# Zero products in TensorE's waits, halves side by side in the feed-forward, and the order of sums and norm steps

## What is computed

```python
# first block, per layer l (x: sequence, y: context)
hx = _rmsnorm(x, norm_g[l]) * (1.0 + scale) + shift      # scale, shift, gate: silu(c) @ w_mod[l] + b_mod[l]
f_in, f_gate, g_u, g_v, g_gate, c_q, c_kv, k_rope, a_gate = _split_in(h @ w_in)
f_out = (_fourier(f_in) @ w_fmix) * silu(f_gate)
g_out = _spatial_gate(g_u, g_v, g_ln_g, g_ws, g_bs) * silu(g_gate)
q  = _rmsnorm(c_q, q_a_g) @ w_uq                          # latents: their sums of squares
kv = _rmsnorm(c_kv, kv_a_g) @ w_ukv
x  = x + gate * (concat([fx, gx, attention * silu(ax)]) @ w_out[l])

# second block
u = a * sigmoid(b)                                        # a, b from x @ w_in
u = depthwise_conv(u, conv_w) + conv_b                    # 31 taps
y_conv = silu(layer_norm(u, conv_ln_g, conv_ln_b)) @ w_conv_out
merged = g_attn * y_attn + g_conv * y_conv                # y_attn: dilated window attention, three groups
x = layer_norm(alpha * x + merged @ w_o, ln1_g, ln1_b)
x = layer_norm(alpha * x + (silu(x @ w_gate) * (x @ w_up)) @ w_down, ln2_g, ln2_b)
```

## Time and profile before

| what | value |
|---|---|
| median of 3 runs | 924.92 us |
| the profiled execution | 929.94 us |
| its span, first to last instruction | 928.1 us |
| mean granted clock of TensorE | 0.983 |
| TensorE busy | 879.0 us, 95% |
| TensorE weight loads | 724.3 us, 78% |
| VectorE busy | 612.8 us, 66% |
| ScalarE busy | 427.1 us, 46% |
| DMA, mean over the span | 147 GB/s |

### The profile page before, as it was taken

One profiled execution on the slowest core, in us unless ns is written; L12 is line 12 of the kernel. 1 busy time (PEld: TensorE's weight loads), 2 busy tenths in 40 slices (PEclk: granted clock), 3 DMA queues, 4 the chain that ended last, 5 costly groups with the idle time before them and its releaser, 6 DMA issues.

```text
span 928.1 us, 13761 instructions
## 1 busy us (share of the span) xinstructions
PE 879.0 (95%) x5592; PEld 724.3 (78%) x5592; DVE 612.8 (66%) x1200; ACT 427.1 (46%) x711; POOL 21.2 (2%) x16
## 2 busy tenths in 40 slices
PE   4899999999999999999999999988999799999996
PEld 1468477767687767877998888887999699999995
DVE  3442666575845759865699999967586845544555
ACT  3342515544633355554544444556453744444441
POOL 0000000000000000000003113000000000000000
PEclk9999999999999999999999999989999899999999
DMA  9666352100263033203555665522366255455541
GB/s 349 261 226 245 143 215 84 46 23 1 91 249 120 12 125 137 83 21 136 162 190 177 200 192 173 158 81 69 101 199 218 73 195 188 172 186 204 178 163 46
DMA packets 39999, 136.71 MB, mean 147 GB/s; under 512 B 4352, under 2 KB 4480, under 8 KB 39680
## 3 DMA queue, kind: packets, MB, share of 16 engines
q1 hardware_dynamic: 38928, 130.48, 41.1%
q10 hardware_dynamic: 1008, 5.36, 1.5%
HBM read 134.77 MB, written 1.05 MB: 146 GB/s over the span
## 4 chain that ended last, share of the span: by engine, by line
PE 79%; DVE 15%; ACT 3%; issue 1%; DMA 1%; DVEq 0%; SPq 0%; ACTq 0%
PE ps L349 9%; PE ps L350 9%; PE ps L354 8%; PE ps L903 6%; PE ps L419 4%; PE ps L421 4%; PE ps L420 4%; PE ps L447 3%; PE ps L679 3%; DVE wlo L1391 2%; PE ps L377 2%; PE ps L702 2%; PE ps L379 2%; PE ps L378 2%; PE ps L366 2%; PE ps L368 1%
## 5 line engine op out<-in xcount | busy, mean ns | idle before, releaser
L1391 DVE TENSOR_TENSOR wlo<-raw,whi 128x1024 fp32r<-128x1024 f32 (+2 forms) x204 | 233.8, 1159 | 38.4 <-ACT whi L941 38.3
L941 ACT ACTIVATE whi<-raw 128x1024 fp32r<-128x1024 f32 (+2 forms) x204 | 204.4, 1005 | 104.0 <-DMA raw<-wpack 46.9
L349 PE MATMUL ps<-hh,whi 128*128 128x256 f32 (+1 forms) x736 | 217.3, 295 | 3.0 <-ACT AF L1264 2.5
L350 PE MATMUL ps<-hl,whi 128*128 128x256 f32 (+1 forms) x736 | 213.4, 290 | 0.0
L354 PE MATMUL ps<-hh,wlo 128*128 128x256 f32 (+1 forms) x640 | 185.7, 290 | 0.0
L349 PEld LDWEIGHTS ps<-hh,whi 128*128 128x128 f32 x736 | 141.9, 193 | 8.3 <-issue 4.8
L350 PEld LDWEIGHTS ps<-hl,whi 128*128 128x128 f32 x736 | 142.0, 193 | 3.0 <-issue 0.7
L354 PEld LDWEIGHTS ps<-hh,wlo 128*128 128x128 f32 x640 | 123.4, 193 | 1.4
L419 PE MATMUL ps<-whi,hh 128*128 128x512 f32 (+1 forms) x192 | 70.8, 369 | 0.2 <-ACT acc L1007 0.2
L420 PE MATMUL ps<-wlo,hh 128*128 128x512 f32 (+1 forms) x192 | 70.2, 366 | 0.0
L421 PE MATMUL ps<-whi,hl 128*128 128x512 f32 (+1 forms) x192 | 70.2, 366 | 0.0
(11 more groups left out here) (267 smaller groups left out, 1554.5 us busy)
## 6 DMA issues: line engine op xcount, KB each, us to landing
raw<-wpack SPq DMA_DIRECT2D x178, 512.0 KB, 4.1
AF<-wmod SPq DMA_DIRECT2D x48, 512.0 KB, 6.1
raw<-wpack SPq DMA_DIRECT2D x24, 256.0 KB, 2.7
XT<-xin SPq DMA_DIRECT2D x4, 512.0 KB, 6.1
raw<-wpack SPq DMA_DIRECT2D x4, 432.0 KB, 5.1
uq<-wuq ACTq DMA_DIRECT2D x2, 768.0 KB, 5.7
cst<-cpack ACTq DMA_DIRECT2D x1, 1093.0 KB, 8.0
AF<-wukv ACTq DMA_DIRECT2D x2, 512.0 KB, 7.0
```

The source lines that it names most:

```text
L349: e.matmul(o, wh[:, b], xh(k), start=j == 0, stop=False, skip_group_check=True)
L350: e.matmul(o, wh[:, b], xl(k), start=False, stop=False, skip_group_check=True)
L941: e.activation(W.hi(i), W.raw(i), ACT.Copy).then_inc(*HI.up(j))
L1391: e.tensor_tensor(W.lo(i), W.raw(i), W.hi(i), ALU.subtract).then_inc(*LO.up(j))
```

## The change

It has five parts.

1. `keep(n)` issues n products of a zeroed 128 x 256 tensor `K.zero` into a PSUM bank that nobody reads: 15 before the first product, 5 behind `mod_t(0, 0)`, 11 behind the first layer norm's sums. VectorE zeroes the tensor first of all.
2. The latents' sums are issued from within `lin_tm`, behind its second weight group of three.
3. `hh` and `hl` become two halves of one tensor `hx`. In chunks 1 to 21 of the feed-forward `lin_wide` takes both as one moving operand of 2 x 256 columns, so the high-by-high and high-by-low parts land in two halves of a bank. ScalarE copies the second half out, and VectorE adds the first half to it, for the gate and for the up projection.
4. Steps of the convolution's norm go to later items: sums 3 to 4, mean 3 to 4, centring 4 to 5, squares (ScalarE) 4 to 6, sum of squares 4 to 7, token sums 5 to 8, roots 5 to 8, spread 6 to 9, and `conv_act` is cut into steps of two channel groups each: scale in 10 and 11, tanh in 11 and 12, product in 12 and 13, high part in 13 and 14, low part in 14 and 15. The squares get four buffers in place of two.
5. In layer 0, VectorE's `bias(0, 5)` is done ahead of `kv_take(0, 0)`.

```diff
+    def lin_wide(key, wname, cols, xw):
+
+        free = ps.take(key)
+        c, wh, wl = weights(key, (wname, 0, tuple(range(KD)), cols), KD * P)
+        pe.wait_ge(*free)
+        for k in range(KD):
+            b = slice(k * P, (k + 1) * P)
+            pe.wait_ge(xw(k))
+            e.matmul(ps.ap(key, 512).rearrange("p (s n) -> p s n", s=2), wh[:, b], K.hx[:, :, k, 0:256], start=k == 0, stop=False, skip_group_check=True)
+            i = e.matmul(ps.ap(key, 256), wl[:, b], hh[:, k, 0:256], start=False, stop=k == KD - 1, skip_group_check=True)
+        i.then_inc(*M.up(key))
+        W.given[c] = M.now()
...
-    def lin_tm(key, wname, l, cols, n, xh, xl, tiles, per, xw, side=None):
+    def lin_tm(key, wname, l, cols, n, xh, xl, tiles, per, xw, side=None, mid=None):
...
+            if mid and g == per:
+                mid()
...
+    def keep(n):
+
+        pe.wait_ge(V["zero"], *ps.take("keep"))
+        for _ in range(n):
+            e.matmul(ps.ap("keep", 256), K.zero[:, 0:P], K.zero[:, :], start=True, stop=True, skip_group_check=True)
+
+
+    keep(15)
     pe.wait_ge(K.c0["cst"])
     mod_g(0, 2, 0)
...
     mod_t(0, 0)
+    keep(5)
...
+        lin_tm((l, "gvkr"), "w_in", l, (("gvkr",), 288), 288, XH, XL, tiles, 3, ht, side=(l, "kf") if l else None, mid=latent_sums)
...
-        if i == 3:
+        if i == 4:
             conv_sums()
-        if i == 5:
+        if i == 8:
             token_sums(("cn2",), 2)
-        if i == 6:
+        if i == 9:
             spread(("cn2",), 256)
...
     ln_sums("ln1")
+    keep(11)
...
-            lin(("fg", f), "w_ffn_gate_2", 0, cc, range(KD), x2h, x2l, 256, xt3)
-            lin(("up", f), "w_ffn_up_2", 0, cc, range(KD), x2h, x2l, 256, xt3)
+            lin_wide(("fg", f), "w_ffn_gate_2", cc, xt3)
+            lin_wide(("up", f), "w_ffn_up_2", cc, xt3)
...
+            e.activation(side[:, 0:256], ps.ap(("fg", m), 256, 256), ACT.Copy).then_inc(*A.up(("fgs", m)))
+            ac.wait_ge(V["fga", m])
+            e.activation(K.AF[:, z:z + 256], side[:, 0:256], ACT.Silu).then_inc(*A.up(("fg", m)))
         highs(("up", m))
+        if m:
+            ac.wait_ge(M["up", m])
+            e.activation(side[:, 256:512], ps.ap(("up", m), 256, 256), ACT.Copy).then_inc(*A.up(("ups", m)))
...
+            dv.wait_ge(A["fgs", m])
+            e.tensor_tensor(side[:, 0:256], side[:, 0:256], ps.ap(("fg", m), 256), ALU.add).then_inc(*V.up(("fga", m)))
+            ps.give(("fg", m), V.now())
+            dv.wait_ge(A["ups", m])
+            e.tensor_tensor(side[:, 256:512], side[:, 256:512], ps.ap(("up", m), 256), ALU.add).then_inc(*V.up(("upa", m)))
+            ps.give(("up", m), V.now())
+            dv.wait_ge(V.now(), A["fg", m], V["f", m - 2] if m >= 2 else None)
+            e.tensor_tensor(h, K.AF[:, z:z + 256], side[:, 256:512], ALU.mult).then_inc(*V.up(("fu", m)))
...
+        for m in range(4):
+            if i == 10 + m // 2:
+                conv_scale(m)
+            if i == 12 + m // 2:
+                conv_silu(m)
+            if i == 14 + m // 2:
+                conv_low(m)
```

More of the change, by code:

```diff
@@ L552, in layer, with latent_sums @@
             pe.wait_ge(*ps.take((l, "kf")))
[L553 to L563, removed]
+        def latent_sums():
+            pe.wait_ge(*free_st, A[l, "cqsq", 1])
+            for t in tiles:
+                for m in range(2):
+                    j = (t - tiles[0]) * P
+                    i = e.matmul(ps.ap(st, 1, t), K.sq[:, m * 512 + j:m * 512 + j + P], C("ones", 0, 1), start=m == 0, stop=m == 1, skip_group_check=True)
+            i.then_inc(*M.up((l, "cqsum")))
+            pe.wait_ge(A[l, "ckvsq"])
+            for t in range(4):
+                i = e.matmul(ps.ap(st, 1, 4 + t), K.acc[:, t * P:(t + 1) * P], C("ones", 0, 1), start=True, stop=True, skip_group_check=True)
+            i.then_inc(*M.up(st))
+        lin_tm((l, "gvkr"), "w_in", l, (("gvkr",), 288), 288, XH, XL, tiles, 3, ht, side=(l, "kf") if l else None, mid=latent_sums)
         ps.drop(st)
@@ L1359, in scalar_program @@
         highs(("fg", m))
+        side = K.AF[:, 8192 + 2 * z:8704 + 2 * z]
         ac.wait_ge(M["fg", m], V["fu", m - 2] if m >= 2 else None)
-        e.activation(K.AF[:, z:z + 256], ps.ap(("fg", m), 256), ACT.Silu).then_inc(*A.up(("fg", m)))
-        ps.give(("fg", m), A.now())
+        if m == 0:
+            e.activation(K.AF[:, z:z + 256], ps.ap(("fg", m), 256), ACT.Silu).then_inc(*A.up(("fg", m)))
+            ps.give(("fg", m), A.now())
+        else:
+            e.activation(side[:, 0:256], ps.ap(("fg", m), 256, 256), ACT.Copy).then_inc(*A.up(("fgs", m)))
+            ac.wait_ge(V["fga", m])
+            e.activation(K.AF[:, z:z + 256], side[:, 0:256], ACT.Silu).then_inc(*A.up(("fg", m)))
         highs(("up", m))
+        if m:
+            ac.wait_ge(M["up", m])
+            e.activation(side[:, 256:512], ps.ap(("up", m), 256, 256), ACT.Copy).then_inc(*A.up(("ups", m)))
         ac.wait_ge(V["fu", m], M["fd", m - 8, 1] if m >= 8 else None)
@@ L1461, in make_h @@
         h_low(l, ks[-1])
+    e.memset(K.zero, 0.0).then_inc(*V.up("zero"))
     e.memset(K.c32[:, :], 0.0).then_inc(*V.up("c32z"))
@@ L1658, in heads_T @@
             ps.give(key, V.now())
+        if l == 0:
+            bias(0, 5)
         kv_take(0, 0)
         if l == 0:
-            bias(0, 5)
             hsum("k", 0, 0, 0, 0)
@@ L1948, in vector_program @@
                 add_up(g.CV[:, k, :], k == 0, ("cn", "acc"), M["h", 1, "s"])
-        if i == 4:
+        if i == 5:
             conv_centre()
-        if i == 5:
+        if i == 7:
+            conv_squares()
+        if i == 8:
             rstd(("cn2",), 2, 512, LN_EPS)
-        if i in (7, 8, 9, 10):
-            conv_act(i - 7)
+        for m in range(4):
+            if i == 10 + m // 2:
[4 more added lines that the diff above has]
+                conv_low(m)
         if i == 12:
@@ L2019, in vector_program @@
         h = K.AF[:, 512 + z:768 + z]
[L2020 to L2022 removed]
+        side = K.AF[:, 8192 + 2 * z:8704 + 2 * z]
+        if m == 0:
+            dv.wait_ge(M["up", m], A["fg", m])
+            e.tensor_tensor(h, K.AF[:, z:z + 256], ps.ap(("up", m), 256), ALU.mult).then_inc(*V.up(("fu", m)))
+            ps.give(("up", m), V.now())
+        else:
+            dv.wait_ge(A["fgs", m])
[3 more added lines that the diff above has]
+            e.tensor_tensor(side[:, 256:512], side[:, 256:512], ps.ap(("up", m), 256), ALU.add).then_inc(*V.up(("upa", m)))
+            ps.give(("up", m), V.now())
+            dv.wait_ge(V.now(), A["fg", m], V["f", m - 2] if m >= 2 else None)
+            e.tensor_tensor(h, K.AF[:, z:z + 256], side[:, 256:512], ALU.mult).then_inc(*V.up(("fu", m)))
         dv.wait_ge(A["f", m])
```

37 lines of the change are left out of this document (21 added, 16 removed).

## The result

The changed kernel takes 913.63 us (median of 4 runs, 909.82 to 914.79) against 925.03 (4 runs, 924.67 to 926.61), 11.4 us less by the medians. The ratio of the means is 0.9866, 95% interval 0.9835 to 0.9898, or 12.4 us less (9.4 to 15.3). The forecast was 904.0, its range 898 to 911: the sign is right, and the time lies 9.6 us above the forecast. The profiled execution took 914.21. The mean granted clock of the four runs was 0.991, 0.992, 0.991 and, in the run of 909.82, 0.995: one of the four had clearly less low clock than the profiled one.

What follows compares the result with a forecast made beforehand. TensorE, busy nearly all the span, was taken as the bound, losing time to half rate and waits; -5.2 - 0.5 - 1.7 - 1.7 - 8.2 - 3.6 = -20.9 took 929.94 to 909.0, the median 924.92 to 904.0, range 898 to 911.

Steps and rivals of the forecast that it cites:

- The norm: Convolution's norm, items 3 to 11: later steps remove waits and low clock, -8.2, between -4 and -9.2.
- rival (b): Convolution's norm: VectorE bounds items 5 to 13, price 4.2, giving 908; chance 0.16.
- (c): Opening and gap before the feed-forward: the zeros don't lift the clock, giving 914; chance 0.09.
- the opening's term: Kernel start: 15 zero products bring what follows to full rate, 5.7 saved, 0.5 given back, -5.2.
- (d): Feed-forward: ScalarE and VectorE handovers never overlap, 9.9 an item against 8.5, slower at 937; chance 0.03.
- The halves: Feed-forward, 21 items: three 256-column products become one of 512 and one of 256, 10.5 ns a step, -3.6.
- keep(11): Gap behind the first layer norm's sums: 11 zero products speed the products behind, 0.4 to 0.7, taken as -0.5.
- the bound of -8: Feed-forward halves: the gain if the whole 13 ns of a second start went too.
- my plain row: Feed-forward halves: the plain 512-column product, 0.229 each, taken as the two-range product's cost, giving -3.6.
- the bound from L629: Feed-forward halves: two-range products at 0.891 against 0.86 cost 8 ns more, which leaves -0.8.
- nothing, if the clock falls elsewhere: Latents' sums, layers 0 and 1: the no-gain case against the forecast -1.7 and -1.7.
- Rival (a): Latent sums and convolution's norm: low clock comes back elsewhere, up to 6.7, giving 910.7; chance 0.20.

Runs made afterwards that it cites:

- the earlier trace: The kernel before, unchanged: the profiled execution that the forecast was built on, 929.94 us.
- the repeat: The kernel before, unchanged, profiled once more: 925.16 us, one execution.

## Why the prediction was right or wrong

**Right.** *The norm.* -8.2 forecast, -8.0 measured alone (-6.4 to -9.4); 41 us forecast for items 3 to 11, 39.9 found. The waits of 2.4 and 2.5 are gone, and the new one at the values is 0.7 where I put 1.0. That the two totals agree so closely is partly luck: the profile saves 9.4 in the items and loses 1.0 behind them. *VectorE* has 31.27 of 39.9 busy and TensorE all of it, so rival (b) did not happen. *Zeros lift the clock*: fifteen take 8.24, where at half rate they would take about 12.9 and at full rate about 6.4, so (c) falls. The 5.7 of the opening's term supposed that everything behind the zeros would run at full rate. No row of before showed that; the changed kernel does, with 1.90 for the second two modulation groups (3.62 in the earlier trace rows) and 1.12 for the spread (2.08). How many of the fifteen would go at half rate was an estimate of mine that no row of before shows; 8.24 fits some four of them (8.24 less 15 x 0.43 is 1.8, four times 0.43), with an end at 9.4. *The feed-forward's copies and sums*: VectorE 91.84 and ScalarE 82.80 in 18 items are 5.1 and 4.6 an item (forecast 5.2 and 4.7), and TensorE never waits, so (d) falls. *Layer 1's sums*: -1.7 forecast, -1.6 in the table, and none of the six profiles with the sums in the groups has the fall, against six of the eight with the sums behind them.

Whether zeros would lift the clock at all was open when the prediction was made. The runs answer it: fifteen products took 8.24 to 9.49 with zeros and 8.84 with ones, each far below the 12.9 of half rate.

**Mis-sized.** *The halves*: a step was to fall from 0.359 to 0.349 and measured (8.387 - 2.74) / 16 = 0.353, 6 ns of the 10.5. By the earlier trace rows one start is 10 ns (twice 5.75 / 48 less 2.75 / 12) where I had about 13, and the bound of -8, which uses the 13, would be -7. The direct term, -2.5 over 21 items, lies between my plain row and the bound from L629; 2.1 of it are in the table's 18 items, and the halves alone brought 2.0 in the ratio. *Data in the opening*: I had it that data would not hold the groups back. TensorE waited 2.12 for the first weights behind the zeros, its weight loads 1.01 more for the second group's, up to 12.70, and the first two groups took 2.21 in place of 1.90. The first input came at 19.31, 0.4 later than forecast.

**Wrong: the step that priced low-clock stretches as fixed pieces of the kernel.** I built the sum on one execution and took 5.0 off at the end for the median, but kept as gains the very losses that made this execution late. In the repeat they are not there: the opening's term is -0.9 instead of -5.2 (4.3 missing), and at layer 0's sums no fall existed to be removed. The repeat has the earliest first projection of the five profiles with the old opening; from their mean the term would be -3.0. The runs settle what it is worth: alone, the opening brought 1.0 (12 runs against 29) where I had 5.2. The parts alone, by their ratios, against the forecast:

| part alone | forecast | measured | missing |
|---|---|---|---|
| the opening's zeros | -5.2 | -1.0 | 4.2 |
| the sums, both layers | -3.4 | -2.4 | 1.0 |
| the norm's items | -8.2 | -8.0 | 0.2 |
| the halves | -3.6 | -2.0 | 1.6 |
| sum, without keep(11) | -20.4 | -13.4 | 7.0 |

Together they measured -12.4 by the ratio (-9.4 to -15.3), so the parts alone account for the result within its interval. In all 20.9 less 12.4, or 8.5, is missing, and the opening's term is half of it.

The next two readings set the one profile of the changed kernel against the one repeat. They say what a fall costs where it lands, not what it costs in a usual run.

**Wrong: "nothing, if the clock falls elsewhere" as the worst of the sums.** The clock fell in the middle of the 288-column products, which then start 0.24 apart in place of 0.13. Before, it had fallen on narrower work. The stage costs +2.4 where I had -1.7 (4.1 missing). In the other four profiles with the sums in the middle a shorter fall comes there too, against three of the eight with the sums behind the groups: the move took layer 1's fall away and made one in layer 0 likelier. The sums' measured price alone, -2.4 for both layers, fits -1.7 from layer 1 and little from layer 0.

**Wrong: keep(11).** The zeros stand behind the last sums. The thin part is ahead of them: 0.7 us of products between 701.3 and 704.6, with waits of 0.97 and 1.38. When the clock falls there, it costs 3.0 before the first zero. Forecast -0.5, found +3.0 (3.5 missing). Leaving the zeros out changed nothing that shows. With those waits filled no profile has the fall, but two of four profiles without the filling lack it as well, so that the filling prevents it is likely and not shown. The -0.9 on the first chunk is not the zeros' alone: without them it takes 25.5 in place of 25.4, and VectorE is busy 7.24 of the first 7.60, as I had said.

Between these two executions the account closes: 4.3 + 4.1 + 3.5 missing, 0.6 at the halves with the first chunk, 0.1 in layer 1, less 1.3 more at the norm and 1.4 for a fall at 200 that I had not touched, is 9.9; forecast -20.9, found -11.0. That this is near the 9.6 of the medians is luck in part: 912.4 is a late execution of the changed kernel and 923.4 an early one of before. Rival (a), with a chance of 0.20 and 6.7 us, is in part what happened: the low clock came back in layer 0 and on the layer norm's sums, not in the norm's items and not in layer 1. Its price was too low, since I counted only falls that return, not falls that land on wider work or were never in a usual run.

**What stays open.** What decides that the clock falls. It fell with TensorE busy without a gap (86.4, and near 90 and 196 with the sums back and the waits filled). It spared the same waits in one kernel and hit them in another, and it differed between two executions of the same instructions. The mean granted clocks say that one of the changed kernel's four runs had less low clock than the other three; which falls each had is not on record. The four lowest medians (908.62, 909.25, 909.49, 909.66) can't be put in order. All lie far below the kernel before. The first two are clear of the changed kernel's interval, by little; the other two overlap it.

## What to carry to other kernels

Before a short stretch of low clock is priced, profile the unchanged kernel several times, and count only what every profile shows. Do the same for the changed kernel before its falls are put down to an edit. Zero products behind thin work came too late for it here (912.02 without the eleven, 913.63 with them); the place to try them is in the waits ahead, where five delayed nothing (squares at 704.65 and 704.59) and the median was 909.66. One-column products in short runs between wide work gave the lowest median, 908.62, though the gain over the alternatives isn't clear of the scatter. Spreading a serial norm over items, so that no engine answers another within one, gave what its waits said it would (8.0 of 8.2), and was the one large gain that stood alone.

## What the runs showed of the hardware

- The clock rises for products of zeros as for products of ones: fifteen fp32 products of 256 columns took 8.24 to 9.49 with zeros (seven profiles), 8.84 with ones; at full rate they would take 6.4 (estimated from the 0.86 of the earlier trace rows).
- One and the same kernel had its first projection at 29.8 and at 26.0, and a fall at 94.7 or none; 7 runs of it beside a later set of experiments went from 924.81 to 929.73. The products of the opening that go at half rate differ as well (the second two modulation groups took 3.62 and 1.90). Against the profile with 26.0 the opening's term is -0.9, which should have been an end of its range.
- The changed kernel's profile and that of the same instructions with ones in the tensor differ, up to TensorE's last product, by two low stretches: half of the one in layer 0, and all of the one at the layer norm (sums of squares 6.78 and 3.72), with 912.4 and 907.4 us of span.
- A moving operand in two ranges of 256 columns cost 0.23 from start to start (0.353 a step less the 0.120 of its 256-column product), the rate of a plain 512-column product in the down projection (2.74 / 12).
- Gains at the clock do not simply add: in medians -4.1 and -4.0 alone gave -2.0 together, and then -4.4 with three more zero products at the start. Each is from four runs, which differ by up to 5 us.
